# The recurrent gates of a hybrid block: two rounded parts of each input block stacked on 128 rows, both gates on 128 columns

## The chip, the cores and the metric

The kernel runs on one core of one Trainium2 chip. The metric is the device time of one execution in microseconds (us). TensorE multiplies matrices into PSUM banks, VectorE, ScalarE and GpSimd compute on rows of SBUF and PSUM (128 rows, called partitions), and SyncE (SP) issues most of the DMA transfers. Each engine runs its own queue of instructions in order, and the engines wait for each other by counting semaphores.

## What is computed

A block of a language model for 512 tokens of width 2048, in float32: a norm, one wide projection, a gated linear recurrence on 1024 channels beside an index-selected attention, their gated mix, and an MLP. The change touches the two gates of the recurrence. They are block diagonal: 16 blocks of 64 channels, each with its own 64x64 matrix.

```python
def block_diag_linear(x, w, b):
    xb = x.reshape(B, S, RNN_BLOCKS, RNN_BLOCK_DIM)
    y = jnp.einsum('bsnd,nde->bsne', xb, w).reshape(B, S, C)
    return y + b

r = jax.nn.sigmoid(block_diag_linear(xf, w_r, b_r))
i = jax.nn.sigmoid(block_diag_linear(xf, w_i, b_i))
log_a = -LRU_C * r * jax.nn.softplus(-lam)
a = jnp.exp(log_a)
u = jnp.sqrt(-jnp.expm1(2.0 * log_a)) * i * xf
# h[t] = a[t] * h[t-1] + u[t]
```

## The kernel before

**Numbers in two parts.** TensorE runs on fp32r operands. Each float32 operand is split into its rounded value (hi, a cast on ScalarE) and the rest (lo, a subtraction on VectorE), and a product takes three matmuls: hi by hi, hi by lo, lo by hi. The helper `products` writes them at L2388, L2389 and L2390, so most matmuls of the trace stand under these three lines.

**Weights.** The projection's weights come in units of 1 MB. For each unit SP loads `raw` (L507, two slots, waiting until the unit two before has its rests), ScalarE rounds it into `whi` (L965, in `hi`, called by `next_hi`; it waits for the load and until TensorE is through with the unit two before), VectorE writes `wlo` (L1599, in `next_lo`), and TensorE runs 48 matmuls of 512 columns (`token_unit` or `pair_unit`, which wait for `lo_ready`). Each engine has the order of this work written out by hand, with the other steps between the units. The first unit of the values is called V0 here, the eighth V7 (in the code U_HD to U_HD + 7), and the units of the keys and queries behind them K0, K1, ... (U_KQ and on). A loop over v = 0 to 7 on ScalarE (L1134 and on) and on VectorE (L1878 and on) prepares unit V(v+1) first and then does the recurrence's steps for that v.

**The recurrence.** Its 1024 channels are 8 chunks of 128 rows, two chunks (j = 0, 1) for each i = 0 to 3. A chunk holds two blocks. For each i:

- ScalarE starts the convolution (`lru_first`, L1086) and VectorE adds three taps (`lru_conv`, L1766) into `xcs`;
- ScalarE rounds the result into `yahi` (`lru_parts`, L1098) and VectorE writes the rest into `xclo` (`lru_low`, L1773); `xclo` has room for one i, so L1772 waits until the gate matmuls of i - 1 are done;
- GpSimd loads the blocks of both gates into the diagonal places of `bd` (`load_bd`, L758, 8 DMAs for each i; the other places were cleared once at L748), ScalarE rounds them (`lru_blocks`, L1093), GpSimd takes the rest (`lru_pool`, L828);
- TensorE computes the gates in `lru_gates` (L2539), here called group G0 to G3: for each chunk and gate one product of a 128x128 matrix with two blocks on its diagonal, three matmuls, 12 for each i. G0 runs behind V1, G1 behind V3, G2 behind V5, G3 behind V7;
- ScalarE applies the sigmoids (L1111, L1114), an exponential, a tanh, a square and a root (`lru_gate`, `lru_mult`; each change of function set shows as ACT_TABLE_LOAD), with the rounding of the output of i - 1 in between (L1103);
- VectorE forms the input of the scan and scans (`lru_var`, `lru_scan`, L1792), GpSimd multiplies by the other branch (`lru_out`, L837), VectorE takes the rest (`lru_out_lo`, L1797).

ScalarE's `lru_gate(i)` waits for the scan of i - 1. The order on ScalarE in the loop over v is:

```python
next_hi(U_HD, 4, i, j)           # rounds V(v+1)
if v == 0: lru_first(1); lru_blocks(0); lru_parts(0)
elif v == 1: lru_first(2); lru_parts(1)
elif v == 5: lru_first(3)
elif v % 2 == 0:
    k = v // 2
    lru_blocks(k); lru_gate(k - 1); lru_mult(k - 1)
    if k != 2: lru_parts(2 if k == 1 else 3)
```

On VectorE, behind the rest of V(v+1): v = 1 has `lru_low(0)` and `lru_conv(1)`, v = 2 has `lru_low(1)`, `lru_conv(2)` and `lru_var(0)`, v = 3 `lru_scan(0)`, v = 4 `lru_low(2)`, v = 5 `lru_scan(1)` and `lru_conv(3)`, v = 7 `lru_low(3)` and `lru_scan(2)`.

Of the kernel before, what the change touches and what calls it, by code (L numbers as in the profile page):

```python
# [5 lines left out]
F32 = mybir.dt.float32  # L6
F32R = mybir.dt.float32r
ACT = mybir.ActivationFunctionType
ALU = mybir.AluOpType
# [3 lines left out]
S = 512  # L13
# [70 lines left out]
HALVES = [slice(0, IDX_DIM), slice(IDX_DIM, 2 * IDX_DIM)]  # L84
# [5 lines left out]
PR_GMIX, PR_GMLP, PR_CW, PR_CB, PR_BR, PR_BI, PR_LAM = 0, 16, 32, 64, 72, 80, 88  # L90
# [168 lines left out]
def hybrid_block(nc, x, g_mix, w_in, conv_w, conv_b, w_r, b_r, w_i, b_i, lam, w_br, w_ba, w_out,  # L259
# [31 lines left out]
    yahi = at("yahi", R4, [P, KR, S], F32R)  # L291
# [4 lines left out]
    xcs = [at("xc0", R3 + 16, [P, 2, S], F32), at("xc1", R3 + 24, [P, 2, S], F32), at("xc2", R4 + 32, [P, 2, S], F32)]  # L296
    xclo = at("xclo", R3 + 20, [P, 2, S], F32R)
    bdhi = at("bdhi", R3 + 28, [P, 2, 2, P], F32R)
# [88 lines left out]
    par = at("par", top + 0.5, [P, PR_ROWS], F32)  # L387
# [354 lines left out]
    def _(pool):  # L742
# [2 lines left out]
        pool.affine_select(out=ident[:], in_=ident[:], compare_op=ALU.not_equal, fill=1.0, base=0,  # L745
                           pattern=[[-1, P]], channel_multiplier=1).then_inc(s.ident_ok, 1)
        pool.memset(eps, EPS).then_inc(s.zeros_ok, 1)
        pool.memset(bd[:], 0.0).then_inc(s.zeros_ok, 1)  # L748
        pool.memset(ones[:], 1.0).then_inc(s.zeros_ok, 1)
        for e in range(HEADS):  # L750
            pool.memset(slopes[:, e:e + 1], 2.0 ** (-8.0 * (e + 1) / HEADS)).then_inc(s.zeros_ok, 1)
        pool.wait_ge(s.zeros_ok, 3)

        def load_bd(i):
            for j in range(2):
                for g, w in enumerate((w_r, w_i)):
                    for b in range(2):
                        pool.dma_start(bd[64 * b:64 * b + 64, j, g, 64 * b:64 * b + 64],  # L758
                                       w[0, bass.ds(4 * i + 2 * j + b, 1)].rearrange("a d e -> (a d) e")
                                       ).then_inc(s.bd_in, 16)  # L760
        def spill_y(p):
            pool.wait_ge(s.tok_lo, U_PAIRS + 5 * p + 5)
            for c, v in enumerate((yshi, yslo)):
# [187 lines left out]
    def _(act):  # L951
# [143 lines left out]
        def lru_parts(i):  # L1095
            for j in range(2):
                act.wait_ge(s.lru_c, 6 * i + 4 + j + 1)
                nc.scalar.copy(yahi[:, 2 * i + j, 0:S], xcs[i % 3][:, j]).then_inc(s.lru_hi, 1)  # L1098

        def lru_hi_out(i):  # L1100
            for j in range(2):
# [3 lines left out]
        def lru_gate(i):  # L1105
            if i:
                act.wait_ge(s.lru_v, lru_dve(i - 1, "scan", 1))
            for j in range(2):
                act.wait_ge(s.lru_mm, 2 * i + j + 1)
                c = 2 * i + j  # L1110
                nc.scalar.activation(rr[:, j], aux[2 * j][:], ACT.Sigmoid, bias=par[:, PR_BR + c:PR_BR + c + 1]).then_inc(s.lru_a, 1)  # L1111
            for j in range(2):
                c = 2 * i + j
                nc.scalar.activation(ii[:, j], aux[2 * j + 1][:], ACT.Sigmoid, bias=par[:, PR_BI + c:PR_BI + c + 1]).then_inc(s.lru_a, 1)  # L1114
            for j in range(2):
                c = 2 * i + j
                act.wait_ge(s.lru_a, lru_act(i, "r", j))
                nc.scalar.activation(aa[:, j], rr[:, j], ACT.Exp, scale=nsp8[:, c:c + 1]).then_inc(s.lru_a, 1)
            if i:
                lru_hi_out(i - 1)  # L1120
            for j in range(2):
                c = 2 * i + j
                nc.scalar.activation(th[:, j], rr[:, j], ACT.Tanh, scale=sp8[:, c:c + 1]).then_inc(s.lru_a, 1)
            for j in range(2):
                act.wait_ge(s.lru_a, lru_act(i, "th", j))
                nc.scalar.activation(rr[:, j], aa[:, j], ACT.Square).then_inc(s.lru_a, 1)
# [467 lines left out]
    def _(dve):  # L1594
# [173 lines left out]

        def lru_low(i):
            for j in range(2):  # L1770
                dve.wait_ge(s.lru_hi, 2 * i + j + 1)
                dve.wait_ge(s.lru_mm, 2 * i)  # L1772
                V.tensor_tensor(xclo[:, j], xcs[i % 3][:, j], yahi[:, 2 * i + j].bitcast(F32),  # L1773
                                ALU.subtract).then_inc(s.lru_lo, 1)

        def lru_var(i):
            for j in range(2):
# [599 lines left out]
    def _(pe):  # L2377
# [6 lines left out]
        def products(dst, pairs, first, last):  # L2384

            n = len(pairs)
            for k, (ah, al, bh, bl) in enumerate(pairs):
                T.matmul(dst, ah, bh, start=first and k == 0, stop=False)  # L2388
                T.matmul(dst, ah, bl, start=False, stop=False)  # L2389
                ins = T.matmul(dst, al, bh, start=False, stop=last and k == n - 1)  # L2390
            return ins
# [106 lines left out]
                T.transpose(bank[0][:, 0:PR_ROWS], par_rows[:], ident[0:PR_ROWS, 0:PR_ROWS]).then_inc(s.par_t, 1)  # L2498

        def spread_rs():  # L2500
            pe.wait_ge(s.zeros_ok, 4)
            pe.wait_ge(s.diag_ok, TT)
            for t in range(TT):
                ins = T.matmul(aux[1][:, P * t:P * t + P], ones[:], diag[:, t], start=True, stop=True)
            ins.then_inc(s.rsb_t, 1)
# [33 lines left out]
        def lru_gates(i):  # L2539
            pe.wait_ge(s.bd_lo, i + 1)  # L2540
            if i:
                pe.wait_ge(s.lru_a, lru_act(i - 1, "i", 1))
            for j in range(2):
                pe.wait_ge(s.lru_lo, 2 * i + j + 1)
                for gate in range(2):
                    ins = products(aux[2 * j + gate][:], [(bdhi[:, j, gate], bdlo[:, j, gate],
                                                           yahi[:, 2 * i + j], xclo[:, j])], True, True)
                ins.then_inc(s.lru_mm, 1)

        def pair_unit(n, slot, half, free):  # L2550
# [329 lines left out]
```

## Time and profile before

| | |
|---|---|
| median of 3 runs | 2504.76 us (2504.76 to 2504.91) |
| the profiled execution | 2504.6 us, its span 2502.8 us |
| TensorE busy | 99% of the span |
| VectorE, ScalarE, GpSimd busy | 81%, 52%, 25% |
| granted TensorE clock, mean | 0.999 |

The span goes from the first to the last instruction; the rest of an execution's time lies around it. The profile shows one execution. Engines are PE (TensorE matmul), PEld (its weight load, which runs beside the matmuls), DVE (VectorE), ACT (ScalarE), POOL (GpSimd) and SP (SyncE). A name such as `yahi<-xc` reads "output from input", and L with a number is a line of the kernel. Matmuls are pipelined: the shown length of one overlaps the next, so the distance between two starts tells what one costs.

### The profile page before, as it was taken

The numbers are of one execution on the slowest core, as the hardware profiler recorded it, in microseconds if no ns is written. First come the engines' busy times: TensorE is split into PE (matmuls) and PEld (weight loads), VectorE is DVE, ScalarE is ACT, GpSimd is POOL, SyncE is SP. The second block draws the span as 40 slices with busy tenths as digits, with TensorE's granted clock in tenths as the row PEclk, the third lists the DMA queues.
The fourth block names the chain that finished last, engine by engine and source line by source line (L and its number), as shares of the span: only waits on it lengthen the run. The fifth ranks groups of instructions, "written<-read, shape, count | busy, mean of one in ns | idle before, by whom it ended". The sixth has DMA issues, their size and how long they took to land.

```text
span 2502.8 us, 33406 instructions
## 1 busy us (share of the span) xinstructions
PE 2487.6 (99%) x12100; PEld 2109.9 (84%) x12100; DVE 2039.5 (81%) x2028; ACT 1306.0 (52%) x1622; POOL 621.0 (25%) x455
## 2 busy tenths in 40 slices
PE   9999999999999999999999999999999999999998
PEld 8888888888888888888888888888888888888886
DVE  5868875556479978843599999999999999999997
ACT  6432484344354454433376666666665445544545
POOL 3650131002100000000022233222330554433434
PEclk9999999999999999999999999999999999999999
DMA  6472223222754864454356665666658695545652
GB/s 201 152 269 87 100 89 100 81 74 98 293 194 155 319 245 192 137 161 140 118 171 202 210 194 189 205 208 210 194 190 327 235 310 202 226 160 193 235 219 84
DMA packets 257197, 460.87 MB, mean 184 GB/s; under 512 B 10416, under 2 KB 150288, under 8 KB 243792
## 3 DMA queue, kind: packets, MB, share of 16 engines
q1 hardware_dynamic: 243920, 414.87, 47.6%
q0 software_dynamic: 12928, 44.57, 6.0%
q8 instruction: 60, 0.98, 0.2%
q10 hardware_dynamic: 256, 0.18, 0.0%
q14 instruction: 33, 0.27, 0.0%
HBM read 366.13 MB, written 93.32 MB: 184 GB/s over the span
## 4 chain that ended last, share of the span: by engine, by line
PE 93%; DVE 4%; issue 1%; POOL 1%; ACT 0%; DMA 0%; SPq 0%; DVEq 0%; ACTq 0%; POOLq 0%
PE stream L2388 10%; PE stream L2390 10%; PE stream L2389 10%; PE stream L2779 8%; PE aux L2779 8%; PE aux L2785 4%; PE stream L2785 4%; PE aux L2817 4%; PE aux L2819 4%; PE aux L2818 4%; PE stream L2817 3%; PE stream L2818 3%; PE stream L2819 3%; PE stream L2664 2%; PE stream L2665 2%; PE stream L2666 2%
## 5 line engine op out<-in xcount | busy, mean ns | idle before, releaser
L1599 DVE TENSOR_TENSOR wlo<-raw,whi 128x2048 fp32r<-128x2048 f32 x72 | 172.9, 2402 | 187.3 <-ACT whi L965 187.1
L926 POOL TENSOR_TENSOR hh<-hh,dn_tmp 128x512 f32<-128x512 f32 x112 | 225.9, 2037 | 320.9 <-ACT dn_tmp L1491 320.9
L965 ACT CAST whi<-raw 128x2048 fp32r<-128x2048 f32 x72 | 137.4, 1909 | 231.1 <-PE stream L2390 231.1
L1528 ACT CAST dhi<-d 128x1024 fp32r<-128x1024 f32 x160 | 167.8, 1053 | 167.9 <-PE aux L2819 100.4
L2388 PE MATMUL stream<-uhi,whi 128*128 128x512 f32 (+1 forms) x640 | 243.2, 380 | 0.1
L2389 PE MATMUL stream<-ulo,whi 128*128 128x512 f32 (+1 forms) x640 | 242.3, 379 | 0.0
L2390 PE MATMUL stream<-uhi,wlo 128*128 128x512 f32 (+1 forms) x640 | 242.1, 378 | 0.0
L2321 DVE TENSOR_TENSOR dlo<-d,dhi 128x1024 fp32r<-128x1024 f32 x150 | 216.4, 1460 | 8.0 <-ACT dhi L1528 8.0
L2779 PE MATMUL stream<-sums,uwhi 128*128 128x512 f32 x672 | 185.9, 392 | 0.5 <-ACT states L1401 0.4
L2779 PE MATMUL aux<-sums,uwhi 128*128 128x512 f32 x672 | 185.3, 391 | 0.0
L2817 PE MATMUL stream<-dhi,dsum 128*128 128x512 f32 x448 | 174.4, 389 | 0.6 <-DVE hh L2215 0.6
L2817 PE MATMUL aux<-dhi,dsum 128*128 128x512 f32 x448 | 174.4, 389 | 0.6 <-DVE dlo L2321 0.6
L2819 PE MATMUL stream<-dhi,dsum 128*128 128x512 f32 x448 | 174.3, 389 | 0.0
L2819 PE MATMUL aux<-dhi,dsum 128*128 128x512 f32 x448 | 174.3, 389 | 0.0
L2818 PE MATMUL stream<-dlo,dsum 128*128 128x512 f32 x448 | 174.3, 389 | 0.0
L2818 PE MATMUL aux<-dlo,dsum 128*128 128x512 f32 x448 | 174.3, 389 | 0.0
L1299 ACT CAST ghi<-g 128x1024 fp32r<-128x1024 f32 x100 | 105.3, 1054 | 131.5 <-PE aux L2666 83.5
L1992 DVE TENSOR_TENSOR glo<-g,ghi 128x1024 fp32r<-128x1024 f32 x100 | 121.7, 1222 | 44.9 <-ACT ghi L1299 44.9
L889 POOL TENSOR_TENSOR hs<-h,hs 128x256 f32<-128x256 f32 x31 | 35.0, 1130 | 430.1 <-ACT hs L1438 430.1
L2779 PEld LDWEIGHTS stream<-sums,uwhi 128*128 128x128 f32 x672 | 121.8, 189 | 22.9 <-DVE uwlo L2118 0.7
L2779 PEld LDWEIGHTS aux<-sums,uwhi 128*128 128x128 f32 x672 | 122.1, 189 | 22.0
L2390 PEld LDWEIGHTS stream<-uhi,wlo 128*128 128x128 f32 x640 | 120.2, 188 | 20.3
(386 smaller groups left out, 6632.9 us busy)
## 6 DMA issues: line engine op xcount, KB each, us to landing
d<-in_w_mlp_down SPq DMA_DIRECT2D x64, 1024.0 KB, 7.3
dsum<-sums_d SPq DMA_DIRECT2D x56, 1024.0 KB, 11.1
raw<-in_w_in SPq DMA_DIRECT2D x48, 1024.0 KB, 5.2
g<-in_w_in SPq DMA_DIRECT2D x32, 1024.0 KB, 7.3
up_b<-in_w_mlp_up SPq DMA_DIRECT2D x32, 1024.0 KB, 8.2
up_a<-in_w_mlp_up SPq DMA_DIRECT2D x32, 1024.0 KB, 5.9
gsum<-usum_d SPq DMA_DIRECT2D x28, 1024.0 KB, 9.6
sums_d<-hlo SPq DMA_DIRECT2D x32, 896.0 KB, 4.2
```

The costliest lines, as they stand in the source:

```text
L926: pool.tensor_tensor(v, v, dn_tmp[r][:], ALU.add).then_inc(s.dn_p, 1)
L1528: nc.scalar.copy(dhi[m % 7][:], parts[j]).then_inc(s.half_hi, 1)
L1599: V.tensor_tensor(wlo[slot][:, 0:width], raw[slot][:, 0:width], whi[slot][:, 0:width].bitcast(F32), ALU.subtract).then_inc(s.lo_ready, 1)
L2321: V.tensor_tensor(dlo[m % 7][:], parts[j], dhi[m % 7][:].bitcast(F32), ALU.subtract).then_inc(s.half_lo, 1)
L2388: T.matmul(dst, ah, bh, start=first and k == 0, stop=False)
L2389: T.matmul(dst, ah, bl, start=False, stop=False)
L2390: ins = T.matmul(dst, al, bh, start=False, stop=last and k == n - 1)
L2779: ins = T.matmul(both(q), uwhi[k][:, q], both_parts(q, j), start=opens and q == 0, stop=closes and q == KP - 1, skip_group_check=True)
L2785: ins = T.matmul(dst, uwlo[k][:, q], shi[q][:, j], start=False, stop=closes and q == KP - 1, skip_group_check=True)
L2817: T.matmul(dst, sh, wh, start=opens and i == 0, stop=False, skip_group_check=not opens)
L2818: T.matmul(dst, sh, wl, start=False, stop=False, skip_group_check=not opens)
L2819: ins = T.matmul(dst, sl, wh, start=False, stop=i == 3, skip_group_check=not opens)
```

## The change

The two blocks of a chunk are computed apart. For block b (0 or 1) of a chunk, one operand of 128 rows holds the rounded values of its 64 channels on one half and their rests on the other half: block 0 in `yahi`, block 1 in `xclo`. The weight operand of 128 rows holds the block's matrices twice, once for each half of the rows; its 128 columns are the 64 of one gate and the 64 of the other. One matmul with the rounded weights gives w_hi (x_hi + x_lo) for both gates, a second with the weights' rests adds w_lo (x_hi + x_lo). So a chunk has 4 matmuls for 6, a group 8 for 12.

Around it: `bd` has no places that stay zero, so L748 goes and each of the 8 DMAs of `load_bd` brings both chunks' 64x64 blocks, twice the bytes in all. ScalarE rounds each block's 64 rows by itself, into `yahi` or `xclo`, and waits for the gate matmuls of i - 1 before (L1772's wait moves from VectorE to ScalarE's `lru_parts`). VectorE writes the rests of 64 rows to the other 64 rows. The two gates of a block stand in two halves of one PSUM bank, so each sigmoid over 128 rows becomes two over 64.

```diff
--- before.py
+++ after.py
@@ -745,19 +745,18 @@
         pool.affine_select(out=ident[:], in_=ident[:], compare_op=ALU.not_equal, fill=1.0, base=0,
                            pattern=[[-1, P]], channel_multiplier=1).then_inc(s.ident_ok, 1)
         pool.memset(eps, EPS).then_inc(s.zeros_ok, 1)
-        pool.memset(bd[:], 0.0).then_inc(s.zeros_ok, 1)
         pool.memset(ones[:], 1.0).then_inc(s.zeros_ok, 1)
         for e in range(HEADS):
             pool.memset(slopes[:, e:e + 1], 2.0 ** (-8.0 * (e + 1) / HEADS)).then_inc(s.zeros_ok, 1)
         pool.wait_ge(s.zeros_ok, 3)
 
         def load_bd(i):
-            for j in range(2):
+            for b in range(2):
                 for g, w in enumerate((w_r, w_i)):
-                    for b in range(2):
-                        pool.dma_start(bd[64 * b:64 * b + 64, j, g, 64 * b:64 * b + 64],
-                                       w[0, bass.ds(4 * i + 2 * j + b, 1)].rearrange("a d e -> (a d) e")
-                                       ).then_inc(s.bd_in, 16)
+                    for rows in HALVES:
+                        pool.dma_start(bd[rows, :, b, HALVES[(g + b) % 2]],
+                                       w[0, 4 * i + b:4 * i + 4:2].rearrange("a d e -> d a e")).then_inc(s.bd_in, 16)
+
         def spill_y(p):
             pool.wait_ge(s.tok_lo, U_PAIRS + 5 * p + 5)
             for c, v in enumerate((yshi, yslo)):
@@ -1095,7 +1094,9 @@
         def lru_parts(i):
             for j in range(2):
                 act.wait_ge(s.lru_c, 6 * i + 4 + j + 1)
-                nc.scalar.copy(yahi[:, 2 * i + j, 0:S], xcs[i % 3][:, j]).then_inc(s.lru_hi, 1)
+                act.wait_ge(s.lru_mm, 2 * i)
+                for b, dst in enumerate((yahi[:, 2 * i + j, 0:S], xclo[:, j])):
+                    nc.scalar.copy(dst[HALVES[b], :], xcs[i % 3][HALVES[b], j]).then_inc(s.lru_hi, 1)
 
         def lru_hi_out(i):
             for j in range(2):
@@ -1108,10 +1109,16 @@
             for j in range(2):
                 act.wait_ge(s.lru_mm, 2 * i + j + 1)
                 c = 2 * i + j
-                nc.scalar.activation(rr[:, j], aux[2 * j][:], ACT.Sigmoid, bias=par[:, PR_BR + c:PR_BR + c + 1]).then_inc(s.lru_a, 1)
+                for b, rows in enumerate(HALVES):
+                    ins = nc.scalar.activation(rr[rows, j], aux[2 * j + b][rows, :], ACT.Sigmoid,
+                                               bias=par[rows, PR_BR + c:PR_BR + c + 1])
+                ins.then_inc(s.lru_a, 1)
             for j in range(2):
                 c = 2 * i + j
-                nc.scalar.activation(ii[:, j], aux[2 * j + 1][:], ACT.Sigmoid, bias=par[:, PR_BI + c:PR_BI + c + 1]).then_inc(s.lru_a, 1)
+                for b, rows in enumerate(HALVES):
+                    ins = nc.scalar.activation(ii[rows, j], aux[2 * j + b][HALVES[1 - b], :], ACT.Sigmoid,
+                                               bias=par[rows, PR_BI + c:PR_BI + c + 1])
+                ins.then_inc(s.lru_a, 1)
             for j in range(2):
                 c = 2 * i + j
                 act.wait_ge(s.lru_a, lru_act(i, "r", j))
@@ -1768,10 +1775,10 @@
 
         def lru_low(i):
             for j in range(2):
-                dve.wait_ge(s.lru_hi, 2 * i + j + 1)
-                dve.wait_ge(s.lru_mm, 2 * i)
-                V.tensor_tensor(xclo[:, j], xcs[i % 3][:, j], yahi[:, 2 * i + j].bitcast(F32),
-                                ALU.subtract).then_inc(s.lru_lo, 1)
+                for b, dst in enumerate((yahi[:, 2 * i + j, 0:S], xclo[:, j])):
+                    dve.wait_ge(s.lru_hi, 4 * i + 2 * j + b + 1)
+                    V.tensor_tensor(dst[HALVES[1 - b], :], xcs[i % 3][HALVES[b], j],
+                                    dst[HALVES[b], :].bitcast(F32), ALU.subtract).then_inc(s.lru_lo, 1)
 
         def lru_var(i):
             for j in range(2):
@@ -2498,7 +2505,7 @@
                 T.transpose(bank[0][:, 0:PR_ROWS], par_rows[:], ident[0:PR_ROWS, 0:PR_ROWS]).then_inc(s.par_t, 1)
 
         def spread_rs():
-            pe.wait_ge(s.zeros_ok, 4)
+            pe.wait_ge(s.zeros_ok, 3)
             pe.wait_ge(s.diag_ok, TT)
             for t in range(TT):
                 ins = T.matmul(aux[1][:, P * t:P * t + P], ones[:], diag[:, t], start=True, stop=True)
@@ -2541,10 +2548,10 @@
             if i:
                 pe.wait_ge(s.lru_a, lru_act(i - 1, "i", 1))
             for j in range(2):
-                pe.wait_ge(s.lru_lo, 2 * i + j + 1)
-                for gate in range(2):
-                    ins = products(aux[2 * j + gate][:], [(bdhi[:, j, gate], bdlo[:, j, gate],
-                                                           yahi[:, 2 * i + j], xclo[:, j])], True, True)
+                pe.wait_ge(s.lru_lo, 4 * i + 2 * j + 2)
+                for b, both in enumerate((yahi[:, 2 * i + j, 0:S], xclo[:, j])):
+                    T.matmul(aux[2 * j + b][:], bdhi[:, j, b], both, start=True, stop=False)
+                    ins = T.matmul(aux[2 * j + b][:], bdlo[:, j, b], both, start=False, stop=True)
                 ins.then_inc(s.lru_mm, 1)
 
         def pair_unit(n, slot, half, free):
```

## Rows read from the trace of the kernel before

**Rows 1.** The page, part 1: busy us (share of the span) xinstructions of each engine.
```profile
PE 2487.6 (99%) x12100; PEld 2109.9 (84%) x12100; DVE 2039.5 (81%) x2028; ACT 1306.0 (52%) x1622; POOL 621.0 (25%) x455
```

**Rows 2.** Waits of TensorE, whole run, longest first: us, times, longest.
```profile
PE aux L2471 <- POOL ident L745: 1.6, 1, 1.6
```

**Rows 3.** Windows: length, then busy us of PE, PEld, DVE, ACT, POOL; PEclk, DMA.
```profile
311.00:335.50 24.50, 24.50 (x109) 20.28 (x108) 17.05 (x19) 21.39 (x27) 8.36 (x10) 1.00 0.28 92
...
360.00:384.50 24.50, 24.50 (x110) 20.30 (x109) 17.33 (x20) 20.03 (x27) 3.07 (x3) 1.00 0.28 87
```

**Rows 4.** Timeline of TensorE: start, us, engine, line: first matmuls of V2, V4, V7, K0.
```profile
311.03 0.39 PE L2388 MATMUL stream<-whi,uhi 128*128 128x512 f32 x1
...
335.51 0.39 PE L2388 MATMUL stream<-whi,uhi 128*128 128x512 f32 x1
...
370.87 0.39 PE L2388 MATMUL stream<-whi,uhi 128*128 128x512 f32 x1
...
384.47 0.39 PE L2388 MATMUL stream<-uhi,whi 128*128 128x512 f32 x1
```

**Rows 5.** Timeline of ScalarE, 300 to 375 us; [idle before <-releaser].
```profile
300.65 1.28 ACT L1098 CAST yahi<-xc 128x512 fp32r<-128x512 f32 x2 [4.77 <-DVE xc L1766]
...
301.84 1.90 ACT L965 CAST whi<-raw 128x2048 fp32r<-128x2048 f32 x1
...
311.80 1.91 ACT L965 CAST whi<-raw 128x2048 fp32r<-128x2048 f32 x1
...
314.24 1.28 ACT L1111 ACT_TABLE_LOAD   x1
...
316.69 1.27 ACT L1114 ACTIVATE lru_ii<-aux,par 128x512 f32<-128x512 f32 x2
...
326.28 1.91 ACT L965 CAST whi<-raw 128x2048 fp32r<-128x2048 f32 x1
...
348.46 1.90 ACT L965 CAST whi<-raw 128x2048 fp32r<-128x2048 f32 x1
...
372.94 1.13 ACT L1098 CAST yahi<-xc 128x512 fp32r<-128x512 f32 x2
...
373.97 1.91 ACT L965 CAST whi<-raw 128x2048 fp32r<-128x2048 f32 x1
```

**Rows 6.** Timeline of VectorE, 305 to 410 us.
```profile
305.98 1.29 DVE L1773 TENSOR_TENSOR xclo<-xc,yahi 128x512 fp32r<-128x512 f32 x2
...
328.21 2.29 DVE L1599 TENSOR_TENSOR wlo<-raw,whi 128x2048 fp32r<-128x2048 f32 x1 [4.54 <-ACT whi L965]
...
332.83 2.34 DVE L1792 TENSOR_TENSOR_SCAN lru_th<-lru_aa,lru_ii 128x512 f32<-128x512 f32 x2
...
350.38 2.29 DVE L1599 TENSOR_TENSOR wlo<-raw,whi 128x2048 fp32r<-128x2048 f32 x1 [3.49 <-ACT whi L965]
...
364.27 2.28 DVE L1599 TENSOR_TENSOR wlo<-raw,whi 128x2048 fp32r<-128x2048 f32 x1
...
398.44 2.29 DVE L1599 TENSOR_TENSOR wlo<-raw,whi 128x2048 fp32r<-128x2048 f32 x1 [3.49 <-ACT whi L965]
...
409.62 2.29 DVE L1599 TENSOR_TENSOR wlo<-raw,whi 128x2048 fp32r<-128x2048 f32 x1 [0.73 <-ACT whi L965]
```

**Rows 7.** Timeline of GpSimd, behind the scan of i = 1: two multiplies.
```profile
356.37 3.75 POOL L837 TENSOR_TENSOR xc<-lru_th,rg 128x512 f32<-128x512 f32 x2 [10.67 <-DVE lru_th L1792]
```

**Rows 8.** Instructions of L758 on GpSimd: ns min/median/max, first and last start.
```profile
L758 POOL DMA_DIRECT2D bd<-in_w_rg_i x16: 522/533/574, 21.5 to 345.2; - x16
```

**Rows 9.** The page, part 6: DMA issues, KB each, us to landing.
```profile
raw<-in_w_in SPq DMA_DIRECT2D x48, 1024.0 KB, 5.2
```

**Rows 10.** Instructions by line: ns min/median/max: 64-row and narrower forms.
```profile
L1053 ACT CAST iq<-stream x16: 470/474/477, 54.9 to 147.1; 64x384 fp32r<-64x384 f32 x16
...
L1705 DVE TENSOR_TENSOR iq<-stream,iq x16: 550/556/560, 56.9 to 149.4; 64x384 fp32r<-64x384 f32 x16
...
L1172 ACT CAST pt<-aux x12: 384/390/593, 458.3 to 619.1; 128x256 fp32r<-128x256 f32 x8, 128x512 fp32r<-128x512 f32 x4
```

## The prediction

> **What bounds the kernel now.** I read the page's busy shares first: TensorE is busy 2487.6 of 2502.8 us [rows 1]. Then TensorE's own waits: the longest in the whole run is 1.6 us, at the very start [rows 2]. So TensorE sets the time, and two things count only: how long it issues, and whether it ever finds its data late. Third, the windows of the stretch that the change touches: a window of 24.5 us holds 24.5 us of TensorE, while VectorE is busy for 17 us of it and ScalarE for 20 to 21 [rows 3]. They have little room, and their queues run in order.
>
> The stretch has eight value-projection units, V0 to V7, and four gate groups, G0 to G3, behind V1, V3, V5 and V7; behind G3 come the first units of keys and queries, K0 to K3. On TensorE V2 starts at 311.03, V4 at 335.51, V7 at 370.87 and K0 at 384.47 [rows 4]. From V2 to V4 are 96 unit matmuls and G1's 12, 108 in 24.48 us: 0.2267 us each. (Their shown length of 0.39 overlaps the next.) A unit is 48 x 0.2267 = 10.88 us, a group 2.72.
>
> A unit needs a rounding of its weights on ScalarE (L965, 1.9 us) and then a rest on VectorE (L1599, which starts 1.93 us behind the rounding's start and takes 2.3). The slack of each is small: V4's rest starts at 328.21 [rows 6] and ends at 330.5, 5.0 us before V4. V7's ends at 364.27 + 2.29, 4.3 us before V7.
>
> **The change, part by part.**
>
> *TensorE.* A group has 8 matmuls for 12, of the same 128 rows and 512 columns: 4 x 4 x 0.2267 = 3.6 us less in all, 0.91 a group. That is the most that it can gain, and it is 0.15%; a measurement of this kernel can tell about 0.2%, 5 us, from no change.
>
> *ScalarE.* Each rounding of L1098 becomes two on 64 rows, each sigmoid of L1111 and L1114 too: 2 more casts and 4 more sigmoids for each i. Does half the rows cost half the time? A 64x384 cast takes 0.474 us, a 128x256 one 0.39 and a 128x512 one 0.593; a 64x384 subtraction on VectorE takes 0.556 [rows 10]. A 128x384 cast would be about 0.49, so the time goes by columns. I take the full step of each: (373.97 - 372.94) / 2 = 0.515 for a cast, (316.69 - 314.24 - 1.28) / 2 = 0.58 for a sigmoid [rows 5]. Per i that is 1.03 + 2.3 us.
>
> *VectorE.* Each subtraction of L1773 becomes two, 0.60 us a step (two in 1.29, [rows 6]): 1.2 us per i.
>
> *A new wait.* xclo now gets half of the rounded values, from ScalarE. So the casts for i wait until group i-1 is through on TensorE. Behind them in ScalarE's queue stand all later weight roundings. For i = 1 (G0 done) and i = 3 (G2 done) other work is later than that. For i = 2 it is not: these casts stand at v = 2, ahead of V4's rounding, and G1 runs directly before V4. V4's weights can't be started before G1 is done.
>
> *GpSimd and queues.* The clear of bd goes, at the start, where nothing waits for it. The block loads stay 8 for each i, with twice the bytes; one takes 0.53 us of GpSimd to issue [rows 8]. If that doubled, 8 would be 4.3 us later, and the cast that needs them comes over 10 us behind them: nothing. The weight loads of SP's queue wait for the rest of the unit two before and land 5.2 us later [rows 9]; with the times below each still lands before its rounding is reached.
>
> Now the replay, queue by queue, from rows 4 to 6:
> - G0. Four casts from 300.65: V2's rounding at 302.9 for 301.84, its rest over at 307.1, four subtractions to 309.5. G0's second half wants them at 308.31 + 0.91 = 309.2: 0.3 late. V2 starts at 310.4, V3 at 321.3.
> - V3. The convolution of i = 1 and its casts end 2.2 + 1.0 us later: V3's rounding at 315.0 for 311.80, in time. The table load of the first sigmoids at 317.4 for 314.24.
> - V4. Gate work took 12.04 us from that table load to V4's rounding at 326.28, of which 1.03 are casts. 11.0 + 2.3 more brings ScalarE to 330.7. G1 starts at 332.2, ends issuing at 334.0, and with the last one's 0.39 is done at 334.2. Four casts (2.06): rounding at 336.3, rest 338.2 to 340.5. **V4 starts at 340.5 for 335.51**, behind a hole of 6.5 us: 5.0 late.
> - V6. The scan of i = 0 ends 6.96 us behind the start of V4's rest (328.21 to 332.83 + 2.34): 345.2. Gate work waits for it, and takes 11.0 + 1.03 (L1103's casts) + 2.3 = 14.35: V6's rounding at 359.5 for 348.46, rest over at 363.8. G2 is through at 340.5 + 21.76 + 1.81 = 364.1. No hole, V6 4.1 late; but the slack is used up.
> - V7. From the start of V6's rest to that of V7's are 364.27 - 350.38 = 13.9 us, the same 6.96 to the end of a scan and then the convolution of i = 3, beside which GpSimd multiplies [rows 6, 7]; the order stays, so I keep the 13.9. 361.5 + 13.9 = 375.4, over at 377.7. TensorE is ready at 375.0. **Hole of 2.7**, V7 6.8 late.
> - G3. The scan of i = 1 ends at 368.4, gate work at 382.8, four casts to 384.9 (K0's rounding stood at 373.97), K0's rest over at 389.1, subtractions at 390.3 and 391.5. G3 is wanted at 388.6. **Hole of 1.9** with both halves. K0 starts at 392.4 for 384.47: 7.9 late.
> - K2, K3. Scan of i = 2 over at 396.3, gate work at 410.6, K2's rest 412.5 to 414.8; K2 is wanted at 392.4 + 21.76 = 414.2: 0.6 more. K3's rest starts 409.62 - 398.44 = 11.2 behind K2's, at 423.7, and is over at 426.0; wanted at 425.7: 0.3.
>
> Sum: -3.6 for the matmuls, and holes of 0.3 + 6.5 + 2.7 + 1.9 + 0.6 + 0.3 = 12.3, gives +8.7. Where VectorE and GpSimd work side by side their lengths vary (the two multiplies of rows 7 took 3.75 us), so this is not exact to better than 1 us; I lean up by half of that: **+9.2**. From K4 on both engines wait for TensorE again, and the rest of the run moves as a block. The profiled execution took 2504.6 us (span 2502.8), the median of the runs is 2504.76, so they are the same for this purpose: 2504.6 + 9.2 = 2513.8.
>
> **The rivals.**
> 1. *Only the wait hurts.* If a half-row instruction cost half, the two engines would do as much work as before. Then V4's rounding stands at 333.9 + 1.03 + 0.1 = 335.0, V4 starts at 339.2, 3.7 late, later units recover nothing, and G2 and G3 give back 1.8: **+1.9**, within the bound. The two ends of the half-row price are thus +1.9 and +8.7; rows 10 lie at the upper one. Chance 0.07, and 0.09 for something between, near +5.
> 2. *The clock falls in the hole.* The longest wait of TensorE before is 1.6 us and the granted clock is 1.00, 2.4 GHz, in every window of rows 3; no row shows what it does behind 6.5 us of nothing. At 1.2 GHz a matmul would take up to 0.2267 us more. If V4 ran so in full, it would be 48 x 0.2267 = 10.9 us later, but V7 waits for VectorE anyway, and not for V4: the first 2.7 us fall into that hole. So 0 to +8.2 on top of the forecast: **2514 to 2522**. The Trainium skill (TensorE: Matmul & The Clock Gate, "Why this matters for your kernels") warns against gaps without work between bursts of matmuls, because the clock goes back to its lower level; no run here shows it. Chance that it adds over 1 us: 0.13.
> 3. *Nothing is late: the other side.* The weights are prepared far enough ahead (5.0 us at V4) that the reordering is swallowed, and the saved matmuls remain: **-3.6 us, 2501.0**, not slower. It decides at ScalarE's arrival at the casts of i = 2: the wait must be over there with 4.3 us left before V4. The program's order speaks against it, since the wait ends when V4 should start. It needs the rounding of V4 ahead of these casts, which the diff doesn't do. Chance 0.04.
>
> **How the numbers follow.** The forecast has 0.67. Slower by over 0.2% (over 2509.8): it, rival 2, and over half of the middle, 0.86. Within 0.2%: rivals 1 and 3 and the rest, 0.13. Faster would need over 5 us where only 3.6 can be saved: 0.01. The range goes from 2509.0 (the middle case) to 2518.5 (the lower half of rival 2).
>
> **What would show it.** 32 matmuls on the gates' banks for 48. In TensorE's waits a hole of 6 to 7 us before V4, released by VectorE's L1599, and smaller ones before V7 and K2 and in G3. ScalarE's casts of i = 2 waiting for TensorE some 3.5 us. Half-row casts of 0.6 us. After K4 no new waits. I am wrong if the hole at V4 is missing or under 4 us, if the half-row instructions take half, or if the windows behind the hole show a clock under 1.00.

## The result, and the profile after

The changed kernel takes 2523.1 us (median of 6 runs, 2522.5 to 2524.3) where the kernel before takes 2504.8 beside it: a ratio of 1.0074, with a 95% interval of 1.0063 to 1.0084. It is 18.3 us slower. The forecast was 2513.8, slower by 9.2, in a range up to 2518.5: the direction was right, the size half of what came.

The profiled execution took 2523.36 us, its span 2521.5. The page's busy line, against [rows 1]:

```profile
PE 2490.7 (99%) x12084; PEld 2110.4 (84%) x12084; DVE 2046.7 (81%) x2036; ACT 1323.0 (52%) x1646; POOL 625.0 (25%) x454
```

TensorE has 16 matmuls fewer and yet more busy time. Its waits, in the whole run, longest first, against [rows 2] (lines of the changed kernel lie some lines off those of the kernel before; L1606 is the weights' rest, L1780 the inputs' rest, L1838 the scaling of the keys' sums, L2395 to L2397 `products`, L2553 and L2554 the gate matmuls):

```profile
PE stream L2395 <- DVE wlo L1606: 6.9, 1, 6.9
PE stream L2395 <- DVE vf L1838: 5.3, 1, 5.3
PE aux L2553 <- DVE xclo L1780: 3.5, 4, 2.6
```

These three are new and hold 15.7 us; the 1.6 us of the kernel before come next. Now the timeline of TensorE from the end of G1 to the start of V4:

```profile
335.68 0.39 PE L2554 MATMUL aux<-xclo,bdlo 128*128 128x512 f32 x1
343.00 0.79 PE L2395 MATMUL stream<-whi,uhi 128*128 128x512 f32 x1 [6.93 <-DVE wlo L1606]
343.59 0.63 PE L2396 MATMUL stream<-wlo,uhi 128*128 128x512 f32 x1
344.01 0.63 PE L2397 MATMUL stream<-whi,ulo 128*128 128x512 f32 x1
```

V4 should start 0.23 us behind the matmul at 335.68. It starts 7.3 later, and then the matmuls no longer follow at 0.2267 us but at 0.42 to 0.43: half the speed. The windows show the same as a clock (length, busy us of PE, PEld, DVE, ACT and POOL, then PEclk), against [rows 3]:

```profile
335.50:345.00 9.50, 2.57 (x8) 1.76 (x7) 4.35 (x5) 8.74 (x11) 0.00 (x0) 0.65 0.10 20
345.00:350.00 5.00, 5.00 (x16) 3.92 (x15) 5.00 (x4) 3.84 (x6) 3.37 (x2) 0.63 0.46 174
350.00:355.00 5.00, 5.00 (x24) 4.14 (x23) 4.88 (x5) 4.89 (x7) 4.71 (x4) 1.00 0.60 200
420.00:430.00 10.00, 6.50 (x21) 5.25 (x22) 9.62 (x10) 4.06 (x5) 3.28 (x2) 0.66 0.29 99
```

The granted clock is 0.65 and 0.63 of full around the hole and its end, and 1.00 from 350 us on; it falls again between 420 and 430. The rate of the matmuls says which level: 512 columns at 1.2 GHz take 0.427 us. The Trainium skill (TensorE: Matmul & The Clock Gate, "Why this matters for your kernels") warns against idle gaps between bursts of matmuls, because the clock then goes back to its lower level. The trace agrees here: 0.65 and 0.63 behind the hole of 7.1 us.

ScalarE's timeline, against [rows 5]. It shows the first two casts of i = 0 (L1099), the sigmoids of i = 0 (L1113, L1119), the first cast of i = 2, and the roundings of V4 and K0 (L964):

```profile
301.56 0.62 ACT L1099 CAST yahi<-xc 64x512 fp32r<-64x512 f32 x1 [4.78 <-DVE xc L1773]
302.20 0.62 ACT L1099 CAST xclo<-xc 64x512 fp32r<-64x512 f32 x1
...
319.71 1.28 ACT L1113 ACT_TABLE_LOAD   x1
321.01 2.79 ACT L1113 ACTIVATE lru_rr<-aux,par 64x512 f32<-64x512 f32 x4
323.82 2.79 ACT L1119 ACTIVATE lru_ii<-aux,par 64x512 f32<-64x512 f32 x4
...
336.16 0.62 ACT L1099 CAST yahi<-xc 64x512 fp32r<-64x512 f32 x1 [2.16 <-PE aux L2554]
...
338.72 1.90 ACT L964 CAST whi<-raw 128x2048 fp32r<-128x2048 f32 x1
...
388.03 1.91 ACT L964 CAST whi<-raw 128x2048 fp32r<-128x2048 f32 x1
```

Two things are to be seen. A half-row cast starts 0.64 us behind the one before (302.20 - 301.56), and four half-row sigmoids take 2.8 us from first to last, 0.70 each. And the casts of i = 2 wait 2.16 us for TensorE's L2554, G1's last matmul: V4's rounding stands at 338.72, for 326.28 before.

VectorE's timeline, against [rows 6]: the first two subtractions of i = 0, the rests of V4, V7 and K2, the scan of i = 3, and the scaling of K1's sums:

```profile
308.39 0.69 DVE L1780 TENSOR_TENSOR yahi<-xc,yahi 64x512 fp32r<-64x512 f32 x1
309.11 0.69 DVE L1780 TENSOR_TENSOR xclo<-xc,xclo 64x512 fp32r<-64x512 f32 x1
...
340.65 2.29 DVE L1606 TENSOR_TENSOR wlo<-raw,whi 128x2048 fp32r<-128x2048 f32 x1 [8.31 <-ACT whi L964]
...
377.37 2.28 DVE L1606 TENSOR_TENSOR wlo<-raw,whi 128x2048 fp32r<-128x2048 f32 x1
...
415.82 2.29 DVE L1606 TENSOR_TENSOR wlo<-raw,whi 128x2048 fp32r<-128x2048 f32 x1 [3.49 <-ACT whi L964]
...
420.43 2.33 DVE L1799 TENSOR_TENSOR_SCAN lru_th<-lru_aa,lru_ii 128x512 f32<-128x512 f32 x2
422.68 1.26 DVE L1838 TENSOR_TENSOR vf<-stream,rs_b 128x512 f32<-128x512 f32 x2
```

The second hole is the surprise. TensorE at the end of K1 and the start of K2:

```profile
417.78 0.39 PE L2397 MATMUL stream<-uhi,wlo 128*128 128x512 f32 x1
423.50 0.77 PE L2395 MATMUL stream<-uhi,whi 128*128 128x512 f32 x1 [5.33 <-DVE vf L1838]
424.06 0.63 PE L2396 MATMUL stream<-ulo,whi 128*128 128x512 f32 x1
```

K2's weights were ready at 415.82 + 2.29 = 418.1, within 0.1 us of the time when TensorE could have taken them (417.78 + 0.23 = 418.0). K2 started at 423.50, behind L1838, which had to wait for the scan of i = 3 ahead of it in VectorE's queue. K2 writes the bank that L1838 reads; that this bank is the cause is tried below.

Step by step, the starts of the units against the kernel before. Everything from V0 on is 0.91 us late in this execution; in the other profiles below it is between -0.04 and 0.79, in one of them (0.68) with the start of the kernel before untouched, so it is scatter, and I take it off:

| | late by, us | what was added since the line above |
|---|---|---|
| V2 | 0.4 | two waits of G0 of 0.6 and 0.2 and the slower issue around them, less 0.9 for the 4 matmuls |
| V4 | 6.6 | the hole of 7.1, less 0.9 |
| V6 | 8.45 | the low clock in V4, 2.8, less 0.9 |
| K0 | 10.85 | waits in G3 and the slower issue around them, 3.3, less 0.9; V7 has no hole |
| behind K3 | 18.2 | the hole before K2, 5.5, and the low clock in K2, 1.8 |

### The profile page after: what moved, and what is told of

Read it like the earlier page. It is cut to its first block, busy times and chain, and to the rows that moved or that the text cites. A ratio compares the mean times of both kernels' runs of the same rounds, so it can differ in the third digit from the quotient of the medians.

```text
span 2521.5 us, 33405 instructions
## 1 busy us (share of the span) xinstructions
PE 2490.7 (99%) x12084; PEld 2110.4 (84%) x12084; DVE 2046.7 (81%) x2036; ACT 1323.0 (52%) x1646; POOL 625.0 (25%) x454
## 4 chain that ended last, share of the span: by engine, by line
PE 91%; DVE 5%; ACT 2%; issue 1%; POOL 1%; ACTq 0%; POOLq 0%; DVEq 0%
PE stream L2395 9%; PE stream L2396 9%; PE stream L2397 9%; PE stream L2786 8%; PE aux L2786 8%; PE aux L2792 4%; PE stream L2792 4%; PE stream L2824 4%; PE stream L2825 4%; PE stream L2826 4%; PE aux L2824 4%; PE aux L2826 4%; PE aux L2825 4%; PE stream L2673 2%; PE stream L2672 2%; PE stream L2671 2%
## 5 line engine op out<-in xcount | busy, mean ns | idle before, releaser
L1606 DVE TENSOR_TENSOR wlo<-raw,whi 128x2048 fp32r<-128x2048 f32 x72 | 173.8, 2414 | 196.3 <-ACT whi L964 196.2
L964 ACT CAST whi<-raw 128x2048 fp32r<-128x2048 f32 x72 | 137.4, 1909 | 230.7 <-PE stream L2397 230.6
L2395 PE MATMUL stream<-uhi,whi 128*128 128x512 f32 (+1 forms) x640 | 244.1, 381 | 5.4 <-DVE vf L1838 5.3
L2397 PE MATMUL stream<-uhi,wlo 128*128 128x512 f32 (+1 forms) x640 | 242.6, 379 | 0.0
L2395 PEld LDWEIGHTS stream<-uhi,whi 128*128 128x128 f32 x640 | 120.6, 188 | 25.7 <-issue 6.1
```

The costliest lines, as they stand in the source:

```text
L1606: V.tensor_tensor(wlo[slot][:, 0:width], raw[slot][:, 0:width], whi[slot][:, 0:width].bitcast(F32), ALU.subtract).then_inc(s.lo_ready, 1)
```

## The experiments

All ran beside the kernel before, whose median over those runs was 2504.5 us. "Over" means over that, by medians. Two theories stood at first. **Q**: the half-row instructions fill the queues of ScalarE and VectorE, and what stands behind them comes late. **W**: the new wait of the casts is the cause.

**The wait alone.** The kernel before with one line more.

```diff
                 act.wait_ge(s.lru_c, 6 * i + 4 + j + 1)
+                act.wait_ge(s.lru_mm, 2 * i)
                 nc.scalar.copy(yahi[:, 2 * i + j, 0:S], xcs[i % 3][:, j]).then_inc(s.lru_hi, 1)
```

> The kernel before with nothing but the wait of the casts for the gate matmuls of i - 1. Theory Q: one hole of 5 to 6 us before V4, nothing late after it; with a lower clock for the first matmuls behind the hole 8 us over the kernel before, without it 5.6. Theory W: most of the 18 us. A total of 8 for 5.6 is the clock's share.

Measured: 2513.46 us, ratio 1.0034 (1.0022 to 1.0047), 9.0 over. TensorE's first wait:

```profile
PE stream L2389 <- DVE wlo L1600: 5.4, 1, 5.4
```

One hole, before V4, 5.6 us between starts, and V6 is 7.9 late against V0: 2.3 more for the low clock. Nothing after it is late. So the wait alone is worth 8 to 9 us, and not 18.

**The halves alone.** The kernel before, with each cast, sigmoid and subtraction in two; one of them as an example.

```diff
-                nc.scalar.activation(rr[:, j], aux[2 * j][:], ACT.Sigmoid, bias=par[:, PR_BR + c:PR_BR + c + 1]).then_inc(s.lru_a, 1)
+                for rows in HALVES:
+                    ins = nc.scalar.activation(rr[rows, j], aux[2 * j][rows, :], ACT.Sigmoid, bias=par[rows, PR_BR + c:PR_BR + c + 1])
+                ins.then_inc(s.lru_a, 1)
```

> The kernel before with the casts, the sigmoids and the subtractions of the gates each cut into two on 64 rows; no wait, no other matmuls. Theory Q: holes before V4 (about 4 us), V7, in G3 and before K2 (5 us), 15 to 17 us over the kernel before, the largest share of any single part. Theory W: under 4 us over. If a half-row instruction cost half, nothing would change.

Measured: 2520.68 us (2518.6 to 2524.0), ratio 1.0068 (1.0051 to 1.0084), 16.2 over; the profiled execution took 2518.57, 14.0 more than that of the kernel before. Its waits:

```profile
PE stream L2396 <- DVE vf L1839: 3.3, 1, 3.3
PE stream L2396 <- DVE wlo L1605: 3.2, 1, 3.2
PE aux L2396 <- DVE xclo L1780: 2.8, 2, 2.4
```

The same three places as in the changed kernel: V4, the gates, K2; V7, for which a hole was expected too, has none. The clock did not fall in the same places, though: behind the hole in G3 eight matmuls here follow at 0.43 us, which costs 1.7 us, and behind the hole before K2 none does. ScalarE's casts of i = 0 and first sigmoids in this kernel:

```profile
300.60 2.52 ACT L1099 CAST yahi<-xc 64x512 fp32r<-64x512 f32 x4 [4.77 <-DVE xc L1772]
...
319.85 2.78 ACT L1114 ACTIVATE lru_rr<-aux,par 64x512 f32<-64x512 f32 x4
```

Four casts in 2.52, four sigmoids in 2.78, the same steps of 0.63 and 0.70 as in the changed kernel, without any of its other parts. Theory Q holds for the largest share, theory W for the second. They don't add up (9.0 and 16.2 for the parts, 18.3 + 3.6 for the whole without the saved matmuls). The next run says why: in the changed kernel, where the queue is late anyway, taking the wait out gives back only 3 us.

**The wait out of the changed kernel, by a second buffer.**

```diff
-    xclo = at("xclo", R3 + 20, [P, 2, S], F32R)
+    xclos = [at("xclo", R3 + 20, [P, 2, S], F32R), at("xclo1", R3 + 8, [P, 2, S], F32R)]
...
-                act.wait_ge(s.lru_mm, 2 * i)
+                act.wait_ge(s.lru_mm, max(0, 2 * i - 2))
...
```

The casts, the subtractions and the gate matmuls take `xclos[(i + 1) % 2]` where they took `xclo`.

> The changed kernel with a second xclo tile for every second i, so that the casts wait for a group that is long done; the order of all queues is the changed kernel's. Theory Q: ScalarE reaches the casts of i = 2 at its own pace, some 2.2 us earlier than the wait allowed, and everything behind moves by about that: 16 to 17 us over the kernel before. Theory W: the loss goes, 4 us over or less.

Measured: 2520.05 us, ratio 1.006 (1.0044 to 1.0077), 15.5 over, 3 less than the change. The hole at V4 shrinks from 7.1 to 4.8, the others stay (V0 to behind K3: 16.0 for 18.2, so 2.2 of the 3 by the profiles). Theory W falls for the changed kernel, as its main cause.

**The casts of i = 2 behind V4's rounding.**

```diff
                     lru_parts(1)
+                elif v == 3:
+                    lru_parts(2)
...
                     lru_gate(k - 1)
                     lru_mult(k - 1)
-                    if k != 2:
-                        lru_parts(2 if k == 1 else 3)
+                    if k == 3:
+                        lru_parts(3)
```

> The changed kernel with ScalarE's four casts of i = 2 moved behind the rounding of V4, so that the new wait no longer stands ahead of it. Theory Q (the half-row instructions fill ScalarE's and VectorE's queues; the wait is a small part of it): V4's rounding comes 3.5 us earlier, the hole at V4 is 3 to 4 us for 7.1 and the clock may stay up, but V7, G3 and K2 are late by the same queue as before: 15 to 16 us over the kernel before, for 18.3 with the change as it is. Theory W (the new wait is the cause): 4 us over or less.

Measured: 2518.69 us, ratio 1.0055 (1.0038 to 1.0071), 14.2 over. Its two longest waits of TensorE:

```profile
PE stream L2397 <- DVE vf L1840: 5.3, 1, 5.3
PE stream L2397 <- ACT vv L1165: 3.5, 1, 3.5
```

V4 now waits for ScalarE's copies of V3's sums (`vv`), which free its banks and stand behind the moved casts: with that a hole of 3.65 us, as forecast in size but for another reason, and the clock fell behind it too (0.50 in the window from 340 to 345 us). The hole before K2 is the same. By the total theory Q holds here too, theory W (4 over or less) does not.

**K1's scaling ahead of the scan.** On VectorE, in the changed kernel.

```diff
-                lru_scan(3)
                 dve.wait_ge(s.lru_v, lru_dve(2, "lo", 1))
                 dve.wait_ge(s.drained, B_KQ)
...
                 V.tensor_tensor(vf[:, m], stream[m][:], rs_b[:], ALU.mult).then_inc(s.drained, 1)
+            if between is not None:
+                between()
```

`between` is the scan of i = 3, for the first keys alone.

> The changed kernel with VectorE's scaling of K1's sums (which frees the bank that K2 writes) ahead of the scan of i = 3. Theory D (the hole of 5.3 us before K2 is the bank, freed behind the scan, and its clock): the hole shrinks to 1 us or so, to what K2's weights set, and 6 to 7 us of the 18 go: 11 to 12 us over the kernel before. Rival (the hole is set by K2's weights): no change.

Measured: 2516.32 us, ratio 1.0047 (1.003 to 1.0063), 11.8 over, 6.8 less than the change. No hole is left before K2. The bank was the cause of it.

Something else shows in this profile. TensorE idles 2.4 us before G3, less than the 2.7 of the changed kernel's profile, in which no matmul of G3 or K0 is slow. Here seven steps are, from two matmuls before the end of G3 on:

```profile
394.76 0.63 PE L2555 MATMUL aux<-xclo,bdlo 128*128 128x512 f32 x1
395.19 0.63 PE L2396 MATMUL stream<-uhi,whi 128*128 128x512 f32 x1
```

The two kernels don't differ up to there, so where the clock falls is in part a matter of the single execution, and totals of kernels with holes can't be told apart to better than 1 to 2 us.

**The saved matmuls alone.**

```diff
-                    ins = products(aux[2 * j + gate][:], [(bdhi[:, j, gate], bdlo[:, j, gate],
-                                                           yahi[:, 2 * i + j], xclo[:, j])], True, True)
+                    T.matmul(aux[2 * j + gate][:], bdhi[:, j, gate], yahi[:, 2 * i + j], start=True, stop=False)
+                    ins = T.matmul(aux[2 * j + gate][:], bdlo[:, j, gate], yahi[:, 2 * i + j], start=False, stop=True)
```

> The kernel before with two of the three matmuls of each gate product; it leaves out the product of the inputs' rests. The same 16 matmuls fewer as in the change, and nothing else. All theories: the ceiling of the change, -3.6 us, or -2.7 if K2 then waits for its bank.

Measured: 2501.93 us, ratio 0.999 (0.9981 to 1.0), 2.6 less than the kernel before, with an interval that just reaches no change. By the profile K0 starts 3.6 earlier against V0, and then:

```profile
PE stream L2388 <- DVE vf L1831: 0.6, 1, 0.6
```

Even the pure saving loses 0.9 again before K2: the scaling was that close to being late already.

**Whole sigmoids in the changed kernel.**

```diff
-                for b, rows in enumerate(HALVES):
-                    ins = nc.scalar.activation(rr[rows, j], aux[2 * j + b][rows, :], ACT.Sigmoid,
-                                               bias=par[rows, PR_BR + c:PR_BR + c + 1])
-                ins.then_inc(s.lru_a, 1)
+                nc.scalar.activation(rr[:, j], aux[2 * j][:], ACT.Sigmoid, bias=par[:, PR_BR + c:PR_BR + c + 1]).then_inc(s.lru_a, 1)
...
```

The sigmoids of the other gate are changed in the same way.

> The changed kernel with each sigmoid on 128 rows of one bank, 16 instructions fewer on ScalarE (half of the rows take the other gate's sums: the values differ, the work is the same). Theory Q: the four extra sigmoids of each i, 2.8 us, are the largest load: V7 and G3 are no longer late, K2 less: 10 us over the kernel before. Theory W: no change, 18 over.

Measured: 2515.12 us, ratio 1.0046 (1.0029 to 1.0062), 10.6 over, 8 less than the change.

```profile
PE stream L2389 <- DVE wlo L1600: 6.9, 1, 6.9
PE stream L2389 <- DVE vf L1832: 2.2, 1, 2.2
```

The hole at V4 stays at 7.1 between starts, as here it is the wait that sets it; G3's is gone and K2's is 2.3 for 5.5. The cut of the sigmoids costs ScalarE 4 x (8 x 0.70 - 4 x 0.58) = 13.1 us of its time, and it gives back more than the wait (8 us for 3). The cut of the casts and that of the subtractions were not run by themselves.

**Filling the hole before K2**, to see the clock.

```diff
+            if not lag:
+                pe.wait_ge(s.drained, B_KQ)
+                for _ in range(24):
+                    T.matmul(stream[2][:], u_hi[0][:, 0:P], u_hi[0], start=True, stop=True)
             pair_unit(n + 2, U_KQ % 2, 0, d)
```

> The changed kernel with 24 matmuls into a free bank (5.4 us at 0.2267) put into the hole before K2. Theory C (behind that hole the first matmuls run at 1.2 GHz and lose 1.8 us): K2's first matmuls at 2.4 GHz, 1.5 to 2 us less than the changed kernel. Rival (the slow start is something else, such as the bank): no change or slower.

Measured: 2522.21 us, ratio 1.0068 (1.0052 to 1.0085): 0.9 less than the change by medians, which is less than forecast. TensorE's timeline, the 24 filling matmuls and K2's first two, and the windows around them:

```profile
417.97 5.60 PE L2620 MATMUL stream<-uhi 128*128 128x512 f32 x24
423.41 0.39 PE L2395 MATMUL stream<-uhi,whi 128*128 128x512 f32 x1
423.63 0.39 PE L2396 MATMUL stream<-ulo,whi 128*128 128x512 f32 x1
```

```profile
417.00:422.00 5.00, 5.00 (x23) 4.14 (x23) 5.00 (x8) 0.25 (x1) 1.83 (x1) 1.00 0.68 213
422.00:427.00 5.00, 5.00 (x23) 4.14 (x23) 4.72 (x4) 3.82 (x5) 1.49 (x2) 1.00 0.00 0
```

K2's matmuls follow at 0.22 to 0.23 us and the clock stays at 1.00. The time is gained (1.8 us in the changed kernel's K2) and mostly lost again: the scaling was done at 421.7, but the filling ran until 423.4. The total says little by itself, as this profile is ahead of the changed kernel's by 0.7 us at V6 already, with fewer slow matmuls in V4. The steps decide: with the same wait for the bank, but TensorE at work in it, K2 is at full speed, where it was slow in the changed kernel and in the two runs above that kept a hole of 5.5 us there. So the slow start is the clock's answer to the hole, and nothing of the bank.

**The halves grouped.** First halves of both chunks, then second halves, for casts, sigmoids and subtractions.

```diff
-            for j in range(2):
-                ...
-                for b, dst in enumerate((yahi[:, 2 * i + j, 0:S], xclo[:, j])):
+            for b in range(2):
+                for j in range(2):
+                    ...
+                    dst = (yahi[:, 2 * i + j, 0:S], xclo[:, j])[b]
```

> The changed kernel with the half-row casts, sigmoids and subtractions in another order among themselves: the first halves of both chunks, then the second halves. Theory H (an instruction overlaps the end of the one before only where both start at the same row): steps of 0.52 and 0.64 us in turn for the casts, 0.58 and 0.70 for the sigmoids, and 1.5 to 2.5 us less than the changed kernel. Rival (half-row instructions never overlap): steps of 0.64 and 0.70 as before, no change.

Measured: 2521.68 us, ratio 1.0068 (1.0053 to 1.0083), 1.4 less than the change, just under the forecast. ScalarE's two casts of the second halves, and four sigmoids:

```profile
302.00 1.14 ACT L1100 CAST xclo<-xc 64x512 fp32r<-64x512 f32 x2
...
319.70 2.53 ACT L1114 ACTIVATE lru_rr<-aux,par 64x512 f32<-64x512 f32 x4
```

Two casts in 1.14 where two took 0.64 + 0.62 = 1.26, four sigmoids in 2.53 for 2.79. Neighbours of the same half overlap again by 0.12 us or so, neighbours of different halves don't. Theory H holds, by these steps; the total moves by no more than the clock scatters.

**Everything in another order.** The changed kernel's work, with its queues rearranged: on ScalarE

```diff
+        next_hi(U_HD, 4, 0, 2)
+        lru_blocks(1)
+        lru_gate(0, lambda: next_hi(U_HD, 4, 0, 3))
+        lru_mult(0)
+        v_out(0, range(TT))
+        next_hi(U_HD, 4, 1, 0)
+        lru_parts(2)
+        lru_blocks(2)
+        lru_gate(1, lambda: next_hi(U_HD, 4, 1, 1))
...
+        def after_gate_2():
+            next_hi(U_HD, 4, 1, 3)
+            lru_parts(3)
+            v_out(1, (0, 1))
...
+                lru_gate(3, lambda: next_hi(U_KQ, 4, 0, 1))
+                next_hi(U_KQ, 4, 0, 2)
                 lru_mult(3)
```

(what is handed to `lru_gate` runs right behind its sigmoids), and on VectorE the rests in the same places, `lru_low(0)` ahead of V2's rest, K1's scaling ahead of the last variance and scan.

> The changed kernel with every queue in another order and no other work: the roundings of V4, V6, K0 and K2 right behind the sigmoids of the gate work, their rests ahead of what waits for the later gate work, the rests of i = 0 ahead of V2's weights, the casts of i = 2 behind V5's rounding, the casts of i = 3 and two of the value copies ahead of the exponentials, K1's scaling ahead of the scan of i = 3. Theory Q (nothing of the loss is in TensorE or in the half-row instructions themselves, it is what they delay): no hole over 1 us in the stretch, the clock at 1.00, and 1 to 3.6 us less than the kernel before. Rival (ScalarE and VectorE have too much work in the stretch for any order): holes remain somewhere, 3 us or more over.

Measured: 2500.8 us (11 runs, 2500.55 to 2501.5), ratio 0.9985 (0.9976 to 0.9994), 3.7 us less than the kernel before. TensorE's longest wait of the run, and two windows:

```profile
PE aux L2500 <- POOL ident L745: 1.6, 1, 1.6
```

```profile
335.50:360.00 24.50, 24.50 (x110) 20.29 (x109) 16.80 (x17) 24.16 (x32) 9.54 (x12) 1.00 0.31 97
...
384.50:430.00 45.50, 45.50 (x203) 37.66 (x202) 29.46 (x27) 27.76 (x32) 9.11 (x4) 1.00 0.29 93
```

No hole in the stretch, the clock at 1.00, and ScalarE busy for 24.2 of 24.5 us. K0 starts 3.6 us earlier against V0, the whole of the 16 matmuls.

Its control is the same order with the work of the kernel before.

> The kernel before, its matmuls, casts and sigmoids as they were, with the order of the queues of the reordered kernel. It has no holes to fill in the stretch, so all theories say 0 against the kernel before, within 1 us. It is the control for the reordered kernel: what that one gains beyond this is the 16 matmuls.

Measured: 2503.95 us, ratio 0.9999 (0.999 to 1.0008). The order alone gives nothing; the 3.2 us between the two are the matmuls.

## Why the prediction was wrong

Right were: the bound and the ceiling (3.6 us in the stretch); the place, cause and size of the first hole (6.5 forecast, 7.1 measured, behind L1606, with the casts of i = 2 waiting for G1, 2.2 us where some 3.5 were forecast); that G3 waits (1.9 forecast, 3.1 measured); that the loss comes in this stretch alone and stays. V7's hole of 2.7 us did not open. Its rest was late as forecast, over at 377.37 + 2.28 = 379.65 (forecast 377.7), but TensorE, slowed in V4, was not there before 380.2. Rivals 1 and 3 did not come. Rival 2 did, the clock fell, and a hole that neither it nor the forecast had came on top: its 2514 to 2522 fell short too.

**The failed step is "K2, K3"**: "K2 is wanted at 414.2: 0.6 more", and 0.3 for K3. It took K2's start as set by its weights alone. It cost 7.3 us in place of 0.9. K2 also waits for VectorE's scaling of K1's sums, which frees its bank and stands behind the scan of i = 3. The kernel before had shown how close that was. VectorE's timeline there, and TensorE's first matmul of K2:

```profile
403.06 2.33 DVE L1792 TENSOR_TENSOR_SCAN lru_th<-lru_aa,lru_ii 128x512 f32<-128x512 f32 x2
405.31 0.67 DVE L1831 TENSOR_TENSOR vf<-stream,rs_b 128x512 f32<-128x512 f32 x1
```

```profile
406.23 0.40 PE L2388 MATMUL stream<-uhi,whi 128*128 128x512 f32 x1
```

The scaling is over at 405.98, K2 starts at 406.23: 0.25 us of slack, against 5.5 for K2's weights. The replay carried the scan late (by its own numbers it ends at 412.5 + 6.96 = 419.5, which would have put K2 at 420.2, 6 us late and not 0.6) and did not ask who stood behind it. The prediction's own rule, what is queued behind the delayed instruction and who waits for that, was applied to ScalarE's wait and not to VectorE's scan. With the scaling moved ahead of the scan the changed kernel takes 2516.3 us, inside the forecast's range.

**The half-row step was mis-sized.** "I take the full step of each", 0.515, 0.58 and 0.60 us, came from neighbours on the same 128 rows, which overlap by 0.1 us. Alternating halves don't: 0.64, 0.70 and 0.72. That is 4 x 0.125 + 8 x 0.12 = 1.5 us more of ScalarE for each i and 0.5 of VectorE. It makes most of the 1.6 us by which V4 was later than forecast (6.6 for 5.0). From V4 to K0 it makes 2.7 us more, the two gate works, the casts of i = 3 and the subtractions; but this is about covered by an error the other way. The replay put the whole of a gate work behind the scan that it waits for. In the trace its table load stands ahead of that wait (at 345.26, the sigmoids at 347.64), 1.28 us for each of the two. The trace of before had a hint: the casts on 64 rows at L1053 [rows 10] come in pairs for the two halves, and a pair takes 0.97 us there, twice the length of one and no overlap; the prediction had used the length of one only.

**The clock, rival 2**, was priced between 0 and 8.2 on top and given 0.13. The profile shows it twice, 2.8 us in V4 and 1.8 in K2. The rival's text let the first 2.7 us vanish in the hole at V7. That hole was gone indeed, but a part of the loss went around it. ScalarE's rounding of V7 waits until TensorE is through with V5, and the sigmoids of i = 2, on which G3 and K0 hang, stand behind it:

```profile
367.79 1.91 ACT L964 CAST whi<-raw 128x2048 fp32r<-128x2048 f32 x1 [2.91 <-PE stream L2397]
...
371.54 2.79 ACT L1113 ACTIVATE lru_rr<-aux,par 64x512 f32<-64x512 f32 x4
```

```profile
368.11 2.33 DVE L1799 TENSOR_TENSOR_SCAN lru_th<-lru_aa,lru_ii 128x512 f32<-128x512 f32 x2
```

With V4 at full speed this rounding could start 2.8 us sooner, and the sigmoids would wait for the scan alone, which is over at 370.44: they would start 1.1 us sooner. So, by estimate, 1.1 of the 2.8 us reach K0. Two profiles bear it out. The kernel with the scaling moved and the one with the hole filled are the changed kernel up to K1, but lost only 2.1 and 2.0 us in V4. Their V6 is 0.67 and 0.73 us less late than the changed kernel's, and their G3 is less late by the same 0.66 and 0.73. In K2 nothing absorbs the clock, and its 1.8 us stay.

From 8.7 by the replay to 18.2 by the profile: 3.0 up to K0, of which 1.1 are the clock and 1.9 the steps less the table loads; and 6.4 behind it, of which 4.6 are the bank and 1.8 the clock. The bank is the largest term, the clock's 2.9 the second.

## What to carry to other kernels

When a delay is replayed through in-order queues, every instruction behind it has to be asked for all that it releases, banks and buffers as well as weights; a wait with 0.25 us of slack is invisible in the waits of the kernel before and the first to open. Two instructions on half the rows cost more than twice one on all: their time goes by columns, and alternating halves lose the overlap as well. Where TensorE sets the time, work saved on it is worth its full price only if the engines that feed it keep their order of urgency: the same instructions in another order turned 18.3 us of loss into 3.7 of gain.

## What the runs showed of the hardware that I had not expected

- Instructions on ScalarE and VectorE start before the one ahead of them is done if both work on the same rows (casts 0.515 us apart that take 0.62), and don't if one starts at row 0 and the next at row 64 (0.64 apart). Grouping the same halves brings half of it back.
- TensorE's clock fell to 1.2 GHz behind all the longer holes of these profiles (3.65, 4.6, 4.8, 5.5, 5.6, 6.8 and 7.1 us), with 8 to 13 slow steps between matmuls after each of the changed kernel's two. Behind the shorter ones it went either way: slow matmuls behind one hole of 3.4 us (V4 with only the halves cut) and none behind another of 3.4 (K2 there); none behind holes of 2.5 to 2.7 in G3 of the changed kernel and three others, but seven or eight behind holes of 2.6, 2.4 and 2.4 in G3 of three other kernels, two of them the same as the changed one up to there. Whether such a hole costs anything differs from one hole to the next and from one execution to the next.
- VectorE and GpSimd slow each other: a subtraction of 0.69 us took 1.67 (at 321.54) while GpSimd formed the rest of the gate blocks beside it, in 2.88 us where the later ones took 1.74 and 1.73.
